# Row norms behind the column products: one VectorE running sum of squares and two TensorE sums over the partitions in place of eight

## What is computed

```
def rms_norm(x, g):
    x32 = x.astype(jnp.float32)
    y = x32 * lax.rsqrt(jnp.mean(x32 * x32, axis=-1, keepdims=True) + EPS)
    return (y * g.astype(jnp.float32)).astype(x.dtype)
...
    x = x + merged @ w_out
    h = rms_norm(x, ffn_norm)
    gate, up = jnp.split(h @ w_ffn_in, 2, axis=-1)
    return x + (jax.nn.silu(gate) * up) @ w_ffn_out
```

## The kernel before

| place in the program | key | pieces of a column (blocks of 128 rows) | tile of squares | next gain applied |
|---|---|---|---|---|
| end of the first layer's mixer | "out" | one (4) | SQO, in AR1 (the trace's AR) | no |
| layer l = 0 of the second block | ("out2", 0) | two (4, 4) | SQ4, in MQ | yes |
| second half of its feed-forward part | ("ffo", 0, 1) | three (4, 4, 2) | SQ5, in FF | yes |
| layer l = 1 | ("out2", 1) | two (4, 4) | SQ4, in MQ | yes |

## Time and profile before

### The profile page before, as it was taken

The page is one execution under the profiler, slowest core; times in us unless marked ns, Lnnn a source line. Parts: engine busy times, 40 slices in busy tenths (PEclk is TensorE's granted clock), DMA queues, the critical chain, the costliest instruction groups (busy, mean ns, idle before and its releaser), DMA issues.

```text
span 2523.6 us, 28645 instructions
## 1 busy us (share of the span) xinstructions
PE 2320.9 (92%) x11077; PEld 1742.6 (69%) x11077; DVE 1230.3 (49%) x2274; ACT 880.0 (35%) x1538; POOL 361.5 (14%) x273
## 2 busy tenths in 40 slices
PE   7899987789889987899999999999779999999999
PEld 5775666554336765677778888776557777888887
DVE  5543457521114888633544434458885235443343
ACT  4334433311103436544233222334455333332221
POOL 0111123000001542232000000045322310000000
PEclk9999999899999998999999999999989999999999
DMA  8126200279995221221222323222111222223222
GB/s 290 47 65 227 76 26 10 92 283 357 372 382 176 75 67 34 59 61 57 84 91 92 100 93 100 72 91 75 51 42 51 67 67 83 92 92 100 92 92 75
DMA packets 198569, 281.61 MB, mean 112 GB/s; under 512 B 13308, under 2 KB 125732, under 8 KB 198436
## 3 DMA queue, kind: packets, MB, share of 16 engines
q1 hardware_dynamic: 197872, 278.60, 33.1%
q10 hardware_dynamic: 564, 1.18, 0.1%
HBM read 277.65 MB, written 2.10 MB: 111 GB/s over the span
## 4 chain that ended last, share of the span: by engine, by line
PE 71%; DVE 16%; ACT 5%; DMA 5%; issue 2%; SPq 1%; POOL 0%; DVEq 0%; ACTq 0%
PE PS L620 18%; PE PS L622 18%; PE PS L621 17%; PE PS L2223 3%; PE PS L1375 2%; PE PS L2263 2%; DVE AL L2540 2%; DVE AL L821 1%; DVE AL L2539 1%; PE PS L2154 1%; PE PS L680 1%; PE PS L1357 1%; DMA RX<-in_w_up_dram 1%; DVE AL L813 1%; DMA RAW<-in_w_up_dram 1%
## 5 line engine op out<-in xcount | busy, mean ns | idle before, releaser
L620 PE MATMUL PS<-OPH,WHI 128*128 128x512 f32 x1224 | 505.5, 413 | 10.2 <-DVE OPL L1411 7.7
L622 PE MATMUL PS<-OPH,WLO 128*128 128x512 f32 x1224 | 486.4, 397 | 0.0
L621 PE MATMUL PS<-OPL,WHI 128*128 128x512 f32 x1224 | 482.8, 394 | 0.0
L575 ACT ACTIVATE WHI<-RAW 128x1024 fp32r<-128x1024 f32 (+2 forms) x286 | 294.1, 1032 | 465.5 <-PE PS L622 457.0
L608 POOL TENSOR_TENSOR WLO<-RAW,WHI 128x1024 fp32r<-128x1024 f32 (+1 forms) x107 | 252.6, 2366 | 1351.7 <-ACT WHI L575 1348.3
L592 DVE TENSOR_TENSOR WLO<-RAW,WHI 128x1024 fp32r<-128x1024 f32 x179 | 214.7, 1201 | 395.9 <-ACT WHI L575 395.9
L620 PEld LDWEIGHTS PS<-OPH,WHI 128*128 128x128 f32 x1224 | 233.3, 191 | 81.0 <-issue 30.1
L622 PEld LDWEIGHTS PS<-OPH,WLO 128*128 128x128 f32 x1224 | 232.9, 190 | 53.1
L621 PEld LDWEIGHTS PS<-OPL,WHI 128*128 128x128 f32 x1224 | 233.5, 191 | 47.7 <-issue 2.4
L620 PE MATMUL PS<-WHI,OPH 128*128 128x512 f32 (+2 forms) x576 | 241.3, 419 | 13.6 <-POOL WLO L608 5.8
L621 PE MATMUL PS<-WLO,OPH 128*128 128x512 f32 (+2 forms) x576 | 226.6, 393 | 0.0
(11 more groups left out here) (401 smaller groups left out, 3368.7 us busy)
## 6 DMA issues: line engine op xcount, KB each, us to landing
RAW<-in_w_in_dram SPq DMA_DIRECT2D x102, 512.0 KB, 3.5
RAW<-in_w_ffn_in_dram SPq DMA_DIRECT2D x88, 512.0 KB, 3.5
RX<-in_w_gate_dram SPq DMA_DIRECT2D x42, 512.0 KB, 7.2
RX<-in_w_down_dram SPq DMA_DIRECT2D x42, 512.0 KB, 11.4
RAW<-in_w_ffn_out_dram SPq DMA_DIRECT2D x40, 512.0 KB, 3.4
RAW<-in_w_mod_dram SPq DMA_DIRECT2D x36, 512.0 KB, 4.5
RX<-in_w_up_dram SPq DMA_DIRECT2D x32, 512.0 KB, 10.2
RAW<-in_w_up_dram SPq DMA_DIRECT2D x25, 512.0 KB, 9.2
```

The lines of the kernel that those rows point to most:

```text
L575: hi.up(A.e.activation(q.fhi, q.flat, ACT.Copy), ("w", q.i))
L620: T.e.matmul(o, a[0], b[0], start=first, stop=False)
L621: T.e.matmul(o, a[0], b[1], start=False, stop=False)
L622: return T.e.matmul(o, a[1], b[0], start=False, stop=last)
```

## The change

`pe_sum_added` and `squares` are new. Square 0 goes to SQ[0]; all others go to SQ[1], and for places 1 to 6 VectorE adds SQ[1] onto SQ[0] (`dve_square_added`), ahead of its addition of the next place. TensorE sums SQ[0] once, behind place 7, and place 7's own squares from SQ[1] where `pe_sum(key, 7)` stood. ScalarE's wait for the buffer is now for VectorE's addition of the place before.

```
--- before.py
+++ after.py
@@ -360,6 +360,7 @@
     copied = Either(copy_v, copy_a)
     set_v, set_a = signal("set_v"), signal("set_a")
     sq, root, rstd = signal("sq"), signal("root"), signal("rstd")
+    squares = signal("squares")
     scaled, nhi, nlo = signal("scaled"), signal("nhi"), signal("nlo")
     split_a, split_v = signal("split_a"), signal("split_v")
     row_a, row_v, row_p = signal("row_a"), signal("row_v"), signal("row_p")
@@ -2048,11 +2049,33 @@
             nlo.up(V.e.scalar_tensor_tensor(OPL[:, m, :], XT[:, m, :], gain, OPH[:, m, :].bitcast(F32),
                                               ALU.mult, ALU.subtract), (nm, m))
 
-        def dve_add_cols(key, columns, gate, nm=None):
+
+
+        def act_square_added(key, m, SQ):
+            if m >= 2:
+                A.wait_ge(*squares[key, m - 1])
+            sq.up(A.e.activation(SQ[:, min(m, 1), :], XT[:, m, :], ACT.Square), (key, m))
+
+        def dve_square_added(key, m, SQ):
+            if m > 1:
+                V.wait_ge(*squares[key, m - 1])
+            V.wait_ge(*sq[key, m])
+            squares.up(V.e.tensor_tensor(SQ[:, 0, :], SQ[:, 0, :], SQ[:, 1, :], ALU.add), (key, m))
+
+        def pe_sum_added(key, SQ):
+
+            PB[key] = B.one()
+            B.clear(PB[key])
+            T.wait_ge(*squares[key, 6])
+            T.e.matmul(ps(PB[key]), C("ones"), SQ[:, 0, :], start=True, stop=False)
+
+        def dve_add_cols(key, columns, gate, nm=None, SQ=None):
             for c, pieces in enumerate(columns):
                 for i in pieces:
                     dve_lo(i + 3)
                 for m in (2 * c, 2 * c + 1):
+                    if SQ is not None and m >= 2:
+                        dve_square_added(key, m - 1, SQ)
                     dve_add(key, m, gate)
                     if nm and m:
                         dve_gained(nm, m - 1)
@@ -2068,15 +2091,15 @@
                         A.wait_ge(*added[key, m])
                         if nm:
                             act_gained(nm, m)
-                        act_square(key, m, XT, SQ, 512)
+                        act_square_added(key, m, SQ)
             if stat:
                 act_root(key, 512, RST)
 
         def pe_add_cols(key, columns, rhs, operand, SQ, stat):
 
             def after(m):
-                if stat and m:
-                    pe_sum(key, m - 1, SQ, 512)
+                if stat and m == 7:
+                    pe_sum_added(key, SQ)
 
             pe_cols(key, columns, rhs, 512, operand, lambda m: [(added, (key, m))], after)
 
@@ -2097,7 +2120,7 @@
             act_add_cols("out", OUT1, SQO, True)
 
         def dve_out():
-            dve_add_cols("out", OUT1, lambda m: mod[:, 2, m, 0:1])
+            dve_add_cols("out", OUT1, lambda m: mod[:, 2, m, 0:1], None, SQO)
             dve_rstd("out", 512, RST)
 
 
@@ -3179,7 +3202,7 @@
                         dve_merged_low(l, m - 1)
             dve_merged_low(l, 7)
 
-            dve_add_cols(("out2", l), J["out2", l], lambda m: 0.5, ("fn", l))
+            dve_add_cols(("out2", l), J["out2", l], lambda m: 0.5, ("fn", l), SQ4)
 
         def dve_merged_low(l, m):
             V.wait_ge(*mix_a["mt", l, m])
@@ -3271,7 +3294,7 @@
                         V.wait_ge(*glu_a["hi", l, m])
                         glu_v.up(V.e.tensor_tensor(AF[1][:, m % 20, :], SLU[:, j, :], AF[0][:, m % 20, :].bitcast(F32),
                                                    ALU.subtract), ("lo", l, m))
-                dve_add_cols(("ffo", l, f), J["ffo", l, f], None, ("an", 1) if f == 1 and l == 0 else None)
+                dve_add_cols(("ffo", l, f), J["ffo", l, f], None, *((("an", 1), SQ5) if f == 1 and l == 0 else ()))
 
 
         OR = ORM[:, :].rearrange("p (t f) -> p t f", t=4)
```

## The result

The changed kernel takes 2502.1 us in the median (2501.4 to 2504.1, 4 runs), the kernel before 2528.4 us in runs on the same chip (2527.1 to 2534.4). The ratio is 0.9893, with a 95% interval of 0.9876 to 0.991: 27 us (1.1%) faster, with an interval of 23 to 31 us. The profiled execution took 2501.4 us with a span of 2499.9 us; against the profiled execution of before, 2502.5 us were forecast.

A forecast was written before the change was run, and what follows sets the result against it. TensorE, busy for 92% of the span, was taken as the bound. 5.16 + 2 x 5.16 - 0.4 + 7.5 = 22.6 us off the median of 2528.4 gave 2505.8 us, in a range of 2500 to 2512.5.

The forecast's parts named there:

- The 24 sums: Six sums go in each of four stages: 5.16 us each in "out" and both out2 layers, 9.07 in ffo.
- The exposed ends: Stage ends, waiting for the addition of square 6: nothing in "out", 0.2 us per out2 layer, 0.7 in ffo.
- "The moved waits for banks: nothing, 1 us at most either way": Waits for PSUM banks, moved by the change, fall on banks emptied long before: nothing, 1 us at most.
- The sum: Total gain over the four stages: 5.16 + 2 x 5.16 - 0.4 + 7.5 = 22.6 us.
- The cover on VectorE: The other 20 additions hide under TensorE's columns of at least 10.9 us; VectorE's 18.8 of 44 us become some 23.
- rival 4: VectorE becomes the bound, its additions waiting for ScalarE's squares: 49 us against 20.6 removed, 2557 us; chance 0.03.
- Rival 1: Experts' stage behind "out": its transfers swallow the gain of "out", 5.2 us lost, 2511.0 us; chance 0.12.
- Rival 2: Four column ends: TensorE waits 1.3 us at each, 5.2 in all less 1.1 already counted, 2509.9 us; chance 0.10.
- Rival 3: Four stage ends: new waits throw TensorE's clock back to 1.2 GHz, 6.4 us lost, 2512.2 us; chance 0.04.
- The port rule: VectorE's additions may block on GpSimd over shared ports: at worst one waits 1.57 us, ffo gives 6.0, not 7.5.

The follow-up runs named there:

- no_adds: The change with VectorE's 24 additions left out, so the sums hold only the squares of places 0 and 7: 2497.2 us, ratio 0.9883 to the kernel before.
- ffo_only: The kernel before with the change made in the stage ("ffo", 0, 1) alone: 2519.5 us, ratio 0.9972 to the kernel before.
- adds_tripled: The change with two further additions of squares, into an unread tile, ahead of each of the 24: 2526.6 us, ratio 0.9994 to the kernel before.
- rotated: The kernel before with all 112 sum matmuls, ffo's banks chosen so everything behind it up to ("out2", 1) finds the change's banks: 2522.3 us, ratio 0.9985.
- late_sum: The change with the sum over SQ[0] moved, in out2 and ffo, behind the next stage's first piece: 2501.4 us, ratio 0.9908 to the kernel before.
- late_sum2: The same kernel as late_sum, run once more for a single look at its matmul step: 2502.7 us, one run.

## Why the prediction held, and where it did not

**The 24 sums**: right. "out" gives 5.17 for 5.16. In ffo the waits of 1.62 and 0.74 went with the sums, as the step from 1612.57 to 1615.77 had said, and 7.47 came for 7.5.

**The exposed ends**: right in kind, with the chain as forecast. In ffo the wait is 1.58 us where near 1.3 was named. In out2, where I chose 0.2 of 0 to 0.5, no_adds measures 0.64 a layer: the wait is 0.40, and the pair behind it takes 1.10 in place of 0.86. The earlier trace rows had shown that a stalled pair takes longer, and I used that for ffo but not here. So the term of 0.4 for two layers is 1.3.

**"The moved waits for banks: nothing, 1 us at most either way"**: this is the step that failed. They gave 2.2 us by the mark, from a single place 95 us behind the stage. I judged the banks by how long they had been empty within the four stages, and did not follow the rotation into the attention, where the banks of the value rows are held until VectorE comes to its copies. It was a gain by luck: the two late banks move the rotation by two places, and with one place, in ffo_only, the wait of 10.2 us stays.

**The sum**: 21.9 + 2.2 = 24.1 us by the parts; three measurements give 27, 23 and 23. The forecast of 22.6 was low by what the banks gave, less 0.7 us at the ends. The first measurement's 27 is above the parts, too, though its interval (23 to 31) holds them.

**The cover on VectorE**: right in its conclusion for this change (no_adds: 21 of 24 additions cost nothing), wrong in its reason. "A column takes at least 10.9 us (48 matmuls)" doesn't hold in "out", whose columns are 24 matmuls, 5.5 us. And work in a column was the wrong measure: VectorE's idle wait for ScalarE's square counts, too. The point from which rival 4 decides is not VectorE's work in a column passing 10.9 us, but, by the estimate above, one more addition a place in "out"; adds_tripled shows it passed with two.

**Rival 1**: false, the experts' stage kept its length. **Rival 2**: false in size, 2.1 us in all against its 5.2. **Rival 3**: false here; behind waits of 0.40 and 1.58 the pair takes 1.10 both times and the windows stand at a clock of 1.00. What the Trainium skill says of TensorE that idles between groups ("TensorE: Matmul & The Clock Gate", HAM oscillation) does show in adds_tripled. Behind 4.37 and 7.24 us of waiting the same pair takes 2.05 us, and the window from 1296 to 1300 has a granted clock of 0.50, the lower level of 1.2 GHz. In ("out2", 1) a wait as long leaves the pair at 1.10; there the clock falls only behind it, and the next products step by 0.43:

```profile
2152.84 1.10 PE L2072 MATMUL PS<-MQ,cst 128*128 128x512 f32 x2 [4.36 <-DVE MQ L2065]
```

In ffo it waits for 3.04 us and the clock stays at 1.00. **The port rule** of the Trainium skill ("SBUF — State Buffer", SBUF: two separate sides) took nothing here: the addition at 1644.38 starts behind GpSimd's split (1641.83 + 1.59), as forecast, and takes 0.69. What the earlier trace rows hinted at fits the rule better than the prediction saw. VectorE's gained half takes 0.74 us alone. It starts with 0.48 us of GpSimd's split left in before, 0.51 in the change and 0.89 in adds_tripled, and takes 0.29, 0.31 and 0.70 us longer: but for 0.2 us each time, it is held until the split ends (GpSimd's spans are rough). GpSimd and VectorE in adds_tripled:

```profile
1662.51 1.97 POOL L609 TENSOR_TENSOR WLO<-RAW,WHI 128x648 fp32r<-128x648 f32 x1 [0.75 <-ACT WHI L576]
1663.59 1.44 DVE L2049 SCALAR_TENSOR_TENSOR OPL<-XT,VT,OPH 128x512 fp32r<-128x512 f32 x1
```

## What to carry to other kernels

Work taken from the engine that the chain runs on is worth its whole length, and the price of what replaces it is what is exposed behind the last product; both can be read in one trace to a few tenths of a microsecond. The cover of work moved to another engine is that engine's whole trip per tile, its waits for a third engine included, against the time of a tile on the first. And where an edit changes how many banks are taken, or in which order, follow the rotation to the next place where a bank is held for long, however far. In layer 1 it can be had alone, as rotated shows.

## What was not expected of the hardware

A pair of matmuls of the sums takes 0.86 us in a full stream, 1.10 behind waits of 0.40, 1.58 and 3.04 us, and 2.05 behind waits of 4.37 and 7.24. Behind one of 4.36 it takes 1.10 and the products behind it 0.43 a step in place of 0.23: waits of one length meet the fall of the clock at different points.

Matmuls of one shape, with no wait and at a granted clock of 1.00, stepped by 0.2333 us for some 120 us of one execution and by 0.2289 in another of the same program (late_sum and late_sum2). 2.4 us hang on it, and the granted clock doesn't tell the two apart.

Where VectorE's gained half starts while GpSimd's split of weights is still running, it takes longer by nearly what is left of the split: 0.29, 0.31 and 0.70 us for 0.48, 0.51 and 0.89 (before, after, adds_tripled).
